# The last modulation section of a transformer step moved from TensorE to VectorE, in four steps a block of the gate and up product

## The reference, cut to what matters

```python
mod_ctx = silu(c_ctx) @ w_ada + b_ada          # for the 128 prompt tokens
mod_lat = silu(c)     @ w_ada + b_ada          # for the 512 latent tokens
sh1, sc1, g1, sh2, sc2, g2 = split(mod, 6)     # six sections of 2048 columns
h = x * (1 + sc1) + sh1
x = layer_norm(ALPHA * x + g1 * mixer(h), ...)
h = x * (1 + sc2) + sh2
gate, up = split(h @ w_gu, 2)
f = (silu(gate) * up) @ w_down
x = layer_norm(ALPHA * x + g2 * f, ...)        # g2: the last section of the modulation
```

## Time and profile before

| what | us |
|---|---|
| median of 3 runs | 2715.17 |
| lowest and highest | 2713.16, 2719.87 |
| the profiled execution | 2721.88 |
| its span | 2720.1 |
| TensorE busy in the span | 2643.3 |

### The profile page before, as it was taken

The page is one execution under the profiler, slowest core; times in us unless marked ns, Lnnn a source line. Parts: engine busy times, 40 slices in busy tenths (PEclk is TensorE's granted clock), DMA queues, the critical chain, the costliest instruction groups (busy, mean ns, idle before and its releaser), DMA issues.

```text
span 2720.1 us, 37395 instructions
## 1 busy us (share of the span) xinstructions
PE 2643.3 (97%) x16040; PEld 2354.7 (87%) x16040; DVE 1424.9 (52%) x1680; ACT 898.4 (33%) x940; POOL 652.8 (24%) x218
## 2 busy tenths in 40 slices
PE   5999999998999999999999999999999999999997
PEld 3787877797988879999999999999999888888875
DVE  5323232346576457655555545555566354444578
ACT  4333333332311154333333333333333333333343
POOL 0000000000000001344443444344434333333440
PEclk9999999999999989999999999999999999999998
DMA  9775757422463142332233323332334645464566
GB/s 378 281 277 209 272 207 255 153 90 91 176 218 118 64 159 80 108 108 88 93 108 108 96 86 106 108 103 84 101 108 158 239 174 213 174 213 166 208 231 233
DMA packets 179384, 438.11 MB, mean 161 GB/s; under 512 B 9980, under 2 KB 25732, under 8 KB 173076
## 3 DMA queue, kind: packets, MB, share of 16 engines
q1 hardware_dynamic: 176916, 430.48, 45.4%
q10 hardware_dynamic: 2304, 5.24, 0.5%
HBM read 401.83 MB, written 33.85 MB: 160 GB/s over the span
## 4 chain that ended last, share of the span: by engine, by line
PE 62%; DVE 11%; DMA 10%; POOL 10%; issue 4%; ACT 3%; SPq 0%; POOLq 0%; ACTq 0%; DVEq 0%
PE ps L2355 6%; PE ps L2356 6%; PE ps L2357 6%; DMA raw_w<-w_gu_b 5%; PE ps L2278 5%; PE ps L2280 5%; PE ps L2279 5%; PE ps L2031 5%; PE ps L2033 5%; PE ps L2032 5%; POOL raw_w L945 3%; PE ps L2011 3%; DVE w_lo L1666 3%; POOL low L942 2%; POOL raw_w L948 2%
## 5 line engine op out<-in xcount | busy, mean ns | idle before, releaser
L1666 DVE TENSOR_TENSOR w_lo<-raw_w,w_hi 128x1024 fp32r<-128x1024 f32 x264 | 336.6, 1276 | 297.6 <-ACT w_hi L1210 294.7
L1210 ACT ACTIVATE w_hi<-raw_w 128x1024 fp32r<-128x1024 f32 x264 | 270.1, 1054 | 601.0 <-POOL raw_w L951 368.9
L2278 PE MATMUL ps<-x_hi,w_hi 128*128 128x320 f32 x1408 | 435.7, 309 | 1.0 <-DVE w_lo L1666 0.7
L2279 PE MATMUL ps<-x_lo,w_hi 128*128 128x320 f32 x1408 | 435.1, 309 | 0.0
L2280 PE MATMUL ps<-x_hi,w_lo 128*128 128x320 f32 x1408 | 435.1, 309 | 0.0
L942 POOL TENSOR_TENSOR low<-raw_w 128x1024 f32<-128x1024 f32 x41 | 103.7, 2528 | 1098.8 <-DMA raw_w<-w_gu_b 1058.7
L1801 DVE TENSOR_TENSOR x_lo<-low,x_hi 128x2560 fp32r<-128x2560 f32 (+2 forms) x55 | 221.3, 4027 | 262.6 <-ACT x_hi L1303 262.6
L2355 PE MATMUL ps<-w_hi,x_hi 128*128 128x512 f32 x880 | 343.8, 391 | 7.7 <-DVE w_lo L1932 2.8
L2356 PE MATMUL ps<-w_lo,x_hi 128*128 128x512 f32 x880 | 343.1, 390 | 0.0
L2357 PE MATMUL ps<-w_hi,x_lo 128*128 128x512 f32 x880 | 342.9, 390 | 0.0
L2278 PE MATMUL ps<-low_r,w_hi 128*128 128x320 f32 x1072 | 333.0, 311 | 1.5 <-DVE w_lo L1666 1.5
(11 more groups left out here) (238 smaller groups left out, 4362.9 us busy)
## 6 DMA issues: line engine op xcount, KB each, us to landing
raw_w<-w_gu_b SPq DMA_DIRECT2D x180, 512.0 KB, 5.6
low<-w_ada SPq DMA_DIRECT2D x68, 1024.0 KB, 6.9
raw_w<-w_down SPq DMA_DIRECT2D x55, 1024.0 KB, 5.2
low<-hidden_scratch SPq DMA_DIRECT2D x33, 1280.0 KB, 6.0
raw_w<-w_in_b SPq DMA_DIRECT2D x33, 1024.0 KB, 9.1
x_raw<-w_ada SPq DMA_DIRECT2D x25, 1024.0 KB, 15.2
raw_w<-w_out SPq DMA_DIRECT2D x16, 1024.0 KB, 5.1
hidden_scratch<-high SPq DMA_DIRECT2D x44, 320.0 KB, 5.9
```

The lines of the kernel that those rows point to most:

```text
L1210: nc.scalar.activation(weight(0, w), src, ACT.Copy).then_inc(prod_hi, 1)
L1666: nc.vector.tensor_tensor(weight(1, n), src, weight(0, n).bitcast(F32), ALU.subtract).then_inc(prod_split, 1)
L2278: mm(out, wh, version(v, 0, k), start=first and k == 0, stop=False)
L2279: mm(out, wh, version(v, 1, k), start=False, stop=False)
```

## The change

The last section (5) leaves the list `ADA`, so 48 steps are left on TensorE. They skip every third `SLOT`, which spreads their 24 pairs over the same three heads. The section is computed in gate and up on VectorE in 128 steps: 8 chunks of 256 columns with 16 steps each (one for each 128 rows). A step multiplies a 128x256 tile of `w_ada` by a per-partition scalar and adds it to an accumulator, once for each of the two conditioning vectors. In each of the 32 blocks from the third on, four steps follow the remainders of items 3, 4, 5 and 6. The tiles (128 KB) go through two staging places that SyncE fills, each load waiting for the step that frees its place. After 16 steps TensorE sums the accumulators over the partitions with 4 matmuls of two columns in a free part of a bank, ScalarE copies 8 columns, and SyncE stores them with 4 transfers of 128 single elements.

```diff
-ADA = [(2, "row", 0), (4, "col", SC), (3, "col", SH), (5, "row", 1)]
+ADA = [(2, "row", 0), (4, "col", SC), (3, "col", SH)]
+LATE, LATE_FROM, LATE_W = 5, 2, 256
+N_LATE = D // LATE_W
+LATE_STEPS = KT * N_LATE
-N_ADA = 16
+N_ADA = 12
...
+def late_step_of(n):
+    block, at = divmod(n - N_PLAIN, 7)
+    i = 4 * (block - LATE_FROM) + at
+    return i if at < 4 and block >= LATE_FROM and i < LATE_STEPS else None
...
-        if done < ADA_STEPS:
+        seen += item[1] == 0
+        if done < ADA_STEPS and (item == INNER or seen % 3):
...
+        def late_traffic(n):
+            i = late_step_of(n)
+            if i is not None and i + 2 < LATE_STEPS:
+                sp.wait_ge(late_used, i + 1)
+                load_late(i + 2)
...
         for b in range(PLAIN + 1, FB):
+            n = N_PLAIN + 7 * (b - PLAIN - 1)
             load_quad(b + 1, A12)
+            q = late_chunk_after(n, 4)
+            if q is not None:
+                store_late(q)
+            late_traffic(n)
             load_quad(b + 1, A11)
             if b == PLAIN + 1:
                 store_hid(0)
             store_hid(b - 2)
+            late_traffic(n + 1)
             load_quad(b + 1, A21)
+            late_traffic(n + 2)
             load_quad(b + 1, A22)
+            late_traffic(n + 3)
...
+        def late_step(n):
...
+            q, k = divmod(i, KT)
+            dve.wait_ge(late_in[i % 2], 16 * (i // 2 + 1))
...
+            for c in range(2):
+                acc, by = cols(late_acc[c], LATE_W), cond_now[:, k, c:c + 1]
+                if k:
+                    ins = nc.vector.scalar_tensor_tensor(acc, late_stage[i % 2], by, acc, ALU.mult, ALU.add)
+                else:
+                    ins = nc.vector.tensor_scalar(acc, late_stage[i % 2], by, None, ALU.mult)
+            ins.then_inc(late_used, 1)
...
             if n - 1 < N_ITEM:
                 prod_rest(n - 1)
+            late_step(n)
...
+            for j in range(4):
+                at = late_acc[j // 2] + P * (j % 2)
+                ins = mm(ps[:, (n + 5) % 8, HALF + 2 * j:HALF + 2 * j + 2], cols(at, P), cols(C_ONES, 2),
+                         start=True, stop=True)
```

## The result

| | us |
|---|---|
| before, median of 5 (lowest, highest) | 2719.86 (2713.16, 2720.39) |
| after, median of 5 (lowest, highest) | 2832.84 (2825.88, 2839.01) |
| ratio, with its 95% interval | 1.042 (1.040 to 1.045) |
| the profiled execution of after, its span | 2839.01, 2837.1 |

The change costs 113 us, 4.2%, where the prediction had 27 to 32 us and a range that ended at 2783 us. The direction was right and the size was not.

What follows compares the result with a forecast made beforehand. TensorE, busy 97% of the span, was taken as the bound, with a closed round through VectorE, A22's load and Pool 0.49 us a block behind. 2721.9 - 17.5 + 45 + 4 - 6.7 gave 2746.7 us, range 2708 to 2783.

Steps and rivals of the forecast that it cites:

- The small parts: Gate and up: sums over partitions hidden, copies negligible, single-element stores 0 to 8 us on the DMA engines, taken as 4.
- Rival 3: Gate and up: third step's tile arrives late, VectorE waits 1.7 us a block, 54 us more, 2801 us; chance 0.10.
- The round: Gate and up: VectorE, A22's load, Pool and ScalarE loop grows from 24.15 to 26.05 us a block, costing 45 us.
- the 0.9: Gate and up: A22's load, spread out by the steps, takes 4.6 us, 0.9 us less, between bounds of 0 and 1.9.
- The sum without the elements: Whole kernel: all terms together gave 2746.7 us, 31.5 us slower than before, including 4 us for the element stores.
- Rival 1: Gate and up: A22's load shortens to 3.2 us or less, round stays within 24.64 us, 2706.1 us; chance 0.10.
- two rules: Trainium skill figures: 0.33 us per VectorE step instruction, where the prediction took 0.40, and 3.2 us for A22's load.
- The heads: Stage of the heads: 19.5 us of TensorE work leaves, up to about 5 us returns as gaps; gain 17.5 us.
- The sums on TensorE: Gate and up: sums over the partitions take 8.4 us, free while TensorE waits for the round, full cost otherwise.
- the signs named ahead: Profile after: TensorE gaps of some 1.4 us in 32 blocks, A22 issued at 9.0 us, third step not waiting for its tile.

Runs made afterwards that it cites:

- e4: Kernel before with section 5 left out of TensorE and computed nowhere, gate and up unchanged: 2707.0 us, ratio 0.9954.
- e1: Changed kernel with each chunk stored as rows by two transfers of 2x128 instead of four of 128 single elements: 2748.5 us, ratio 1.0105.
- e15: Changed kernel with only two of the four single-element transfers per chunk: 2823.3 us, ratio 1.0382.
- e8: Changed kernel with the four single-element transfers issued behind A22 and the fourth tile instead of ahead of A11: 2751.9 us, ratio 1.0127.
- e5: Kernel before plus only four transfers of 128 single elements in each of eight blocks, between the loads of A12 and A11: 2822.5 us, ratio 1.0369.
- e10: e1 with A11 and the hidden rows' store issued ahead of the first step's wait and tile: 2790.1 us, ratio 1.0265.
- e7: e1 with A22 issued ahead of the third step's wait and tile: 2748.0 us, ratio 1.0112.
- e2: e1 with no tile loaded after the first two, all steps computing on those: 2713.6 us, ratio 0.9983.
- e3: e1 with all tiles loaded and waited for, but a step cut to one instruction of 8 columns: 2730.6 us, ratio 1.0041.

## Why the prediction was wrong, point by point

The accounts of the 113 us: the heads give 12.3 (e4), the steps, tiles and sums in gate and up cost 41.5 (e1 against e4), the elements 84.3 (after against e1).

- **The small parts: the step that failed.** The sentence "what they take of the DMA engines I bound by 0 and 1 us each chunk, up to 8 us, and take 4" was worth 4 us. It was 10.0 us a chunk (36.4 - 26.4) and 84 us in all. With half of the elements it is still 75 us (e15), so it isn't a price for each of them. The bounds had no row behind them, as the prediction says itself ("No row has such a transfer"), and a bound without a row belongs at the cost of the nearest stall, not near zero. The place was misjudged too. That the first step "has it waiting anyway" is true of the 1.85 us of issuing, but behind them in the queue stand a tile and three quarters, all in the round. e8 shows that the place decides, since the same elements cost 3 to 6 us behind A22.
- **Rival 3, the third step's tile.** It had a chance of 0.10 and was to cost 54 us in all blocks. Its mechanism came true in seven of the eight blocks with elements, 9.6 to 12.5 us at a time, and not in the others: there the tiles took 3.6 us, and the third step was due as they came. The two items were priced as independent, and they were not: what slows the loads makes the tile late, and the tile, ahead of A22 in the queue, makes A22 late. But the tile isn't needed for a long block: the eighth has none and takes 36.2 us, and e5 has none at all. e10 shows the same without elements, at 42 us over e1.
- **The round: right size, partly wrong cause.** The block was forecast at 26.05 us and took 26.06 (e1). The parts were right as they stood: a step 0.80 (0.79 measured), A22 issued 9.0 us after item 2 (9.00), last blocks back at 24.6 (24.1 to 24.7). The load of A22 took 5.1 us and not 4.6. But the reason given, that A22's late issue sets the round, fell with e7, where A22 leaves 1.16 us earlier and nothing is gained. e2 beside e7 says it once more: A22 leaves 7.85 and 7.84 us after item 2, and the blocks are 24.94 and 26.10 us. What differs is A21 (5.5 and 6.68 us) and the tiles. In e1 A21 leaves 1.95 us later than before, and Pool starts 2.1 us later. The prediction had 1.9 us for this from other terms, 2.80 us for A22 less 0.9 us, and the 0.9 was the middle of 0 and 1.9 without a row. So the agreement of 26.05 and 26.06 is partly luck. The steps, its largest term, cost no wait by themselves (e2, where 1.6 of their 2.4 us act), and the tiles cost more than it gave them (e3).
- **The sum without the elements.** e1 is 29 us slower than before, where 31.5 were forecast. That is luck too: 5.2 us less from the heads, 3.5 us less in gate and up (41.5 for 45), and the 4 us for the elements, which e1 doesn't have.
- **Rival 1 and two rules.** For an instruction of 128x256 VectorE took 0.40 us, as the row had it, and not the 0.33 us of the Trainium skill (VectorE: DVE Perf Modes, "The TRN2 errata — SBUF-src ops pay a fixed extra latency per instruction"), which says of itself that it runs low. The 3.2 us of a load by the Trainium skill (DMA: Bandwidth & Descriptors, "Anatomy of one DMA — SWDGE (gpsimd) path") did not come either. It is an estimate from a fit that the Trainium skill gives for transfers issued from Pool, and SyncE issues these. With A22 issued last and late (e10), Pool started 4.05 us behind it in the median, the least of all kernels. Rival 1 had 3.2 us as its condition.
- **The heads.** 17.5 us were forecast, 12.3 came. The matmuls went as counted, 128 fewer at 0.12 us and four `adasum`s, 19.5 us. "At most" 5 us of gaps was too low a bound: 3.5 us are seen as gaps, 3.7 us more are missing, part of them perhaps by the clock.
- **The sums on TensorE**, 8.4 us, were held to be hidden while TensorE waits for the round, and to cost all of it otherwise. The second half came true in e2, where nothing covers them: 8.3 us busy, 6.6 us lost. For the first half no run took them away from e1.

Of the signs named ahead, one spoke at once: the third step was not to wait for its tile. It does, for 9.6 to 12.5 us, in nearly one block of four. TensorE's gaps in ordinary blocks were as named, 29.9 us in 28 blocks in e1, some 1.1 us each instead of 1.4.

## What to carry to other kernels

Price a transfer by what is queued behind it and is needed soon, not by its bytes or its issue: 16 KB as single elements cost 84 us ahead of the loads of a closed round and 3 to 6 us behind them. Store a vector that lies across the partitions as rows, by a small product that turns it, or put its store where the queue then rests. And when an idle engine is to be filled, ask first which of its idle time lies beside an engine that it slows, and what the operands of the new work cost on their way in: here the work alone made TensorE wait for nothing, and the operands did.

## What the runs showed of the hardware

- Four transfers of 128 single 4-byte elements made the packets of the loads around them slow, and not by their own time: their packets took 9 ns each, and the 512 packets of 4096 bytes of such a block 207 to 288 us of engine time where it is 102 to 110 us in e1. Two of the four transfers still made a block 8.0 us longer where four made it 10.0.
- Loads of 512 KB queued behind them landed in 16.3 us (median of the block), and in 5.1 us in a block without them.
- Two loads of 512 KB issued 1.2 to 2.4 us apart let Pool start 7.2 to 7.8 us behind the first one's issue (medians of seven kernels), whichever of the spacings it was.
- A split on VectorE (two inputs in SBUF) took 1.22 us alone and 3.0 to 3.3 us beside Pool's sums; four instructions of steps 1.86 and 6.01 us; a sum on Pool 2.4 and 3.2 us.
- After a wait of 4.80 us that ended at 1568.73, TensorE's granted clock was 0.50 between 1570 and 1574 us, its level of 1.2 GHz, and 1.00 again from 1578. In after, TensorE between 1570 and 1574 us, and from 1578 to 1582:

```profile
1570.00:1574.00 4.00, 4.00 (x17) 4.00 (x17) 3.96 (x6) 0.00 (x0) 1.44 (x1) 0.50 0.32 114
1578.00:1582.00 4.00, 4.00 (x28) 3.84 (x27) 0.00 (x0) 0.00 (x0) 3.80 (x2) 1.00 0.00 0
```

Over the span it is 0.975 in after and 0.991 before. Since the round and not TensorE sets the pace in these blocks, the lower clock follows from the waits, and no run gave it a cost of its own.
